# Layer norms of a decoder layer: four last slabs by token tile, scaled rows on ScalarE alone, an early split moved

## The reference

```python
h = layer_norm(ALPHA * h + 0.5 * swiglu(h, ffn1...), ln1_g, ln1_b)      # first norm
mix = hybrid_mixer(h, ...)      # projections, Mamba-2 branch, windowed attention, gates, w_out
h = layer_norm(ALPHA * h + mix, ln2_g, ln2_b)                            # second norm
h = layer_norm(ALPHA * h + 0.5 * swiglu(h, ffn2...), ln3_g, ln3_b)      # last norm

def layer_norm(x, g, b):
    mu = mean(x); xc = x - mu; var = mean(xc * xc)
    return xc * rsqrt(var + 1e-5) * g + b
def swiglu(x, w_gate, w_up, w_down):
    return (silu(x @ w_gate) * (x @ w_up)) @ w_down
```

## Time and profile before

| | us |
|---|---|
| median of 3 runs | 2670.36 |
| time of the profiled execution | 2668.99 |
| its span (first to last instruction) | 2667.4 |
| PE busy | 2634.5 (99%) |
| PE weight loads busy | 2188.8 (82%) |
| DVE busy | 2002.6 (75%) |
| ACT busy | 1361.7 (51%) |
| POOL busy | 130.0 (5%) |
| granted PE clock, mean | 0.996 |

### The profile page before, as it was taken

One profiled execution on the slowest core, in us unless ns is written; L12 is line 12 of the kernel. 1 busy time (PEld: TensorE's weight loads), 2 busy tenths in 40 slices (PEclk: granted clock), 3 DMA queues, 4 the chain that ended last, 5 costly groups with the idle time before them and its releaser, 6 DMA issues.

```text
span 2667.4 us, 36687 instructions
## 1 busy us (share of the span) xinstructions
PE 2634.5 (99%) x12546; PEld 2188.8 (82%) x12546; DVE 2002.6 (75%) x2410; ACT 1361.7 (51%) x1678; POOL 130.0 (5%) x170
## 2 busy tenths in 40 slices
PE   8999999999999999999999999999999999999997
PEld 7888888888787788888888888888878888888886
DVE  6999997688666665677777765444689999977986
ACT  5555555455344454566555554444355555554553
POOL 1000000000000000211111100000000000000000
PEclk9999999999999999999999999999999999999999
DMA  6666566666655546665555565667666665666664
GB/s 224 204 191 209 185 205 204 214 200 204 189 171 147 156 150 197 206 181 179 177 177 177 179 183 165 190 190 247 200 190 204 190 211 186 205 202 229 210 208 171
DMA packets 286195, 513.96 MB, mean 193 GB/s; under 512 B 19648, under 2 KB 52592, under 8 KB 284048
## 3 DMA queue, kind: packets, MB, share of 16 engines
q1 hardware_dynamic: 279552, 485.03, 57.8%
q0 software_dynamic: 4880, 25.36, 2.6%
q10 hardware_dynamic: 1664, 2.26, 0.2%
HBM read 506.23 MB, written 6.36 MB: 192 GB/s over the span
## 4 chain that ended last, share of the span: by engine, by line
PE 95%; DVE 3%; ACT 1%; issue 0%; DMA 0%; POOL 0%; POOLq 0%; SPq 0%; ACTq 0%; DVEq 0%
PE acc L787 13%; PE acc L789 13%; PE acc L788 13%; PE acc L853 5%; PE acc L855 5%; PE acc L854 5%; PE acc L871 4%; PE acc L872 4%; PE acc L873 4%; PE spare L871 4%; PE spare L872 4%; PE spare L873 4%; PE spare L855 3%; PE spare L854 3%; PE spare L853 3%; PE spare L756 2%
## 5 line engine op out<-in xcount | busy, mean ns | idle before, releaser
L1728 DVE TENSOR_TENSOR w_lo<-land,w_hi 128x1024 fp32r<-128x1024 f32 (+1 forms) x956 | 1149.2, 1219 | 499.4 <-ACT w_hi L1309 490.6
L1309 ACT ACTIVATE w_hi<-land 128x1024 fp32r<-128x1024 f32 (+1 forms) x956 | 976.8, 1029 | 916.9 <-PE acc L789 328.0
L787 PE MATMUL acc<-w_hi,a_hi 128*128 128x512 f32 (+1 forms) x1184 | 451.2, 381 | 2.6 <-DVE a_lo L1775 1.8
L789 PE MATMUL acc<-w_hi,a_lo 128*128 128x512 f32 (+1 forms) x1184 | 435.8, 368 | 0.0
L788 PE MATMUL acc<-w_lo,a_hi 128*128 128x512 f32 (+1 forms) x1184 | 434.4, 367 | 0.0
L787 PEld LDWEIGHTS acc<-w_hi,a_hi 128*128 128x128 f32 x1184 | 223.9, 189 | 46.8 <-issue 9.2
L789 PEld LDWEIGHTS acc<-w_hi,a_lo 128*128 128x128 f32 x1184 | 223.6, 189 | 38.2
L788 PEld LDWEIGHTS acc<-w_lo,a_hi 128*128 128x128 f32 x1184 | 224.1, 189 | 37.4 <-issue 3.6
L853 PE MATMUL acc<-w_hi,a_hi 128*128 128x512 f32 x576 | 227.7, 395 | 2.0 <-DVE a_lo L1775 1.7
L855 PE MATMUL acc<-w_hi,a_lo 128*128 128x512 f32 x576 | 225.1, 391 | 0.0
L854 PE MATMUL acc<-w_lo,a_hi 128*128 128x512 f32 x576 | 225.0, 391 | 0.0
(11 more groups left out here) (388 smaller groups left out, 4233.1 us busy)
## 6 DMA issues: line engine op xcount, KB each, us to landing
land<-w_in SPq DMA_DIRECT2D x232, 512.0 KB, 3.9
land<-ffn_w_gate SPq DMA_DIRECT2D x176, 512.0 KB, 3.9
land<-ffn_w_up SPq DMA_DIRECT2D x176, 512.0 KB, 4.3
land<-ffn_w_down SPq DMA_DIRECT2D x176, 512.0 KB, 4.7
land<-w_ssd_o SPq DMA_DIRECT2D x64, 512.0 KB, 4.3
land<-w_in SPq DMA_DIRECT2D x132, 128.0 KB, 2.3
land<-w_attn_o SPq DMA_DIRECT2D x32, 512.0 KB, 4.1
land<-w_out SPq DMA_DIRECT2D x32, 512.0 KB, 4.4
```

The costliest lines, as they stand in the source:

```text
L787: pe.matmul(to, rows_hi, hi, start=first, stop=False)
L789: mm = pe.matmul(to, rows_lo, hi, start=False, stop=last)
L1309: act.activation(w_hi[:, l % SPLIT, 0:deep, 0:width], land[:, l % LAND, 0:deep, 0:width], ACT.Copy).then_inc(high, 1)
L1728: dve.tensor_tensor(w_lo[:, l % SPLIT, 0:deep, 0:width], land[:, l % LAND, 0:deep, 0:width], w_hi[:, l % SPLIT, 0:deep, 0:width].bitcast(F ...
```

## The change

There are four edits.

1. `HALVED` goes from 3 to 4: the last four slabs of the last chunk of down1, out and down2 are gone through by token tile. In down1 and down2 the chunk's last four slabs are the last four of the stage (the four before them belong to the chunk beside it).
2. ACT's `ln_tile` with gain and bias writes the scaled rows into `sz` in float32 (two instructions), and then `a_hi` as a rounding copy of `sz` (one instruction of 128x512), with a wait of ACT for its own writes between them. From tile 2 on it first waits until DVE is done with tile u - 2, whose place in `sz` it takes.
3. DVE's `ln_tile` loses its two scaling instructions and the wait behind them, and takes `sz` as ACT wrote it. Before DVE uses `sz` for other things (`mixed_rows`) it waits for the end of its own tiles 6 and 7.
4. In `ln_first` the split of the next stage's first slab moves behind the normalising of tile 0.

```diff
-HALVED = 3
+HALVED = 4
...
@@ ln_tile of ACT
+                if u >= 2:
+                    read_bank(phase, 0, f"t{u - 2}")
+                h = sz[:, u % 2, :].rearrange("p (k n) -> p k n", k=2)
                 for k in range(2):
-                    last = act.activation(a_hi[:, 2 * u + k, :], two_tiles(bank)[:, k, :], ACT.Identity,
+                    last = act.activation(h[:, k, :], two_tiles(bank)[:, k, :], ACT.Identity,
                                           scale=ln_col[:, cols, 2 * u + k:2 * u + k + 1],
                                           bias=ln_col[:, cols + 1, 2 * u + k:2 * u + k + 1])
-                last.then_inc(tile_hi, 1)
+                ch.link(last)
+                act.activation(a_hi[:, 2 * u:2 * u + 2, :], h, ACT.Copy).then_inc(tile_hi, 1)
...
@@ ln_tile of DVE
                 h = sz[:, u % 2, :].rearrange("p (k n) -> p k n", k=2)
-                for k in range(2):
-                    last = dve.tensor_scalar(h[:, k, :], two_tiles(bank)[:, k, :],
-                                             ln_col[:, cols, 2 * u + k:2 * u + k + 1],
-                                             ln_col[:, cols + 1, 2 * u + k:2 * u + k + 1], ALU.mult, ALU.add)
-                ch.link(last)
                 dve.tensor_tensor(a_lo[:, at, :], h, a_hi[:, at, :].bitcast(F32), ALU.subtract
                                   ).then_inc(bank_out[bank], 1)
...
@@ ln_first of DVE
                     evacuate_half(phase, i, cc, scale, t, no)
+                    dve.wait_ge(ln_p, (no - 1) * TOK + t + 1)
+                    ln_part(t, 0)
+                    ln_part(t, 1)
                     if t == 0:
                         for l in range(EARLY_V):
                             split(after, 0, l)
-                    dve.wait_ge(ln_p, (no - 1) * TOK + t + 1)
-                    ln_part(t, 0)
-                    ln_part(t, 1)
...
@@ mixed_rows of DVE
                 read_done(ln, 0, f"t{u}")
+                if s == 0:
+                    read_done(ln, 0, "t6")
+                    read_done(ln, 0, "t7")
```

## The result

The changed kernel took 2678.87 us (median of 8 runs, 2677.12 to 2684.21); the kernel before took 2670.51 (8 runs). The ratio is 1.0034, with a 95% interval of 1.0025 to 1.0042: slower by 9 us. The forecast was 2669.3, and the time lies outside its range. The profiled execution took 2678.22 us, 9.2 more than that of before.

A forecast was written before the change was run, and what follows sets the result against it. PE was taken as the bound, busy 99% of the span, with only two norm gaps of about 4.4 us to win. Gains of 0.72 and 0.66, cut to 1.1 for the clock, took 2670.36 to 2669.3 us (range 2666.3 to 2671.8).

The forecast's parts named there:

- Parts 2 and 3: Both norms: with the scaling on ACT alone, `a_lo` comes 1.80 us behind ACT's start, not 2.16; gain 0.36 us each.
- the sum: Both norms together: 0.72 us at the first and 0.66 at the second, 1.38 us, taken as 1.1 after the clock.
- The rival on the slower side: ACT at both norms: a tile with its split takes over 3.2 us and PE follows ACT; up to 2679 us; chance 3%.
- ACT's wait for its own writes: ACT, between the scaling and the copy to `a_hi`: taken as 0.04 us, with 0.2 as the upper bound.
- the lag of 0.36: First norm: DVE started tile 1's evacuation 0.36 us later than PE's end allowed; removing this was the gain.
- At the second norm the same stretch: Second norm, to PE's first product: gain 0.3 us from DVE starting tile 1 sooner and 0.36 from the scaling, 0.66.
- PE's wait for `a_lo`: Sign at the first norm: this wait would be near 1.4 us instead of 1.80.
- out's last slabs: End of out: slab 31's `w_lo` ready 0.56 us ahead; rival that PE waits, at most some 0.7 us, 2669.9; chance 5%.
- The clock: Both norms: if its rise ignores PE's work, half the gain is lost; rival that it stays up, 2665.0 or 2667; chance 5%.
- my 0.7 to 1.4: Whole kernel: bounds of the gain in us, by whether the clock's rise stays put or moves with the work.
- one of my signs of being wrong: At the norms: the forecast is wrong if the clock's low stretch changes by more than 1 us.
- Parts 1 and 4: First norm: four slabs by token tile and the moved split let tile 1's evacuation start sooner; gain 0.36 us (0.3 to 0.43).

The follow-up runs named there:

- e1_fill16: The changed kernel with 16 one-column copies more on DVE, spread over the slabs of attn_o ahead of the ssd loop: 2667.74 us, ratio 0.9992.
- e3_parts23: The kernel before with the scaling on ACT alone, HALVED = 3 and the early split where it was: 2678.53 us, ratio 1.0034.
- e4_before_fill113: The kernel before with 113 one-column copies on DVE ahead of the slabs of attn_o, and none of the four edits: 2680.97 us, ratio 1.0043.
- e5_fill2: The changed kernel with 2 one-column copies on DVE ahead of the ssd loop: 2677.9 us, ratio 1.0031.
- e6_fill4: The changed kernel with 4 one-column copies on DVE ahead of the ssd loop: 2667.77 us, ratio 0.9992.
- e9_fill124: The changed kernel with 124 one-column copies on DVE ahead of the ssd loop: 2668.53 us, ratio 0.9996.
- e10_halved4: The kernel before with HALVED = 4 alone: 2668.86 us, ratio 0.9996.
- e13_in116: The kernel before with 116 one-column copies on DVE inside the body of the ssd loop: 2673.26 us, ratio 1.001.

## Why the prediction was wrong, point by point

**The step that failed.** Parts 2 and 3 took the 16 instructions that DVE loses at the first norm for time saved and nothing else ("now DVE saves 2 x 0.99 of scaling"), and the sum had no term for anything outside the norms and the ends of the stages. The missing term is the fetching of DVE's instructions: +11.2 us of PE's time in the profiled execution, shown by e1_fill16 (gone with 16 copies), e3_parts23 (there with that edit alone) and e4_before_fill113 (there without any edit). The Trainium skill has a rule for it ("Runtime: NRT & Kernel Launch", section "Instruction fetch mechanics"): a taken branch whose target isn't in the current window of two pages forces a fetch before execution can go on. The traces agree on the stall, 3.3 to 4.5 us here from the jump to the next instruction. It does not agree on the size of the pages for DVE: the section says 16 KB, 256 instructions, with room for two. The changed kernel and e4_before_fill113 begin their loop exactly 128 instructions apart against such pages, so in one of the two a body of 262 would reach only two of them and stay. Both stall. Here DVE's blocks are 8 KB (0.39 less 0.31 MB for ten), and it is the fourth that is too many.

Why the fourth is too many can be read from the packets, though they don't say which block they bring. In each of the five kernels with gaps there are five fetches from one jump to the next, for a body of four blocks, and the fifth comes 0.2 to 2.1 us before DVE starts the fourth block (in the changed kernel at 1445.52, where DVE starts it at 1446.80). So by the count a block behind the body was fetched before the jump. Where the body has three blocks, it and the one behind make four, and in the kernel before no fetch comes at all between the jumps. The reading that fits all runs is that four blocks stay and that the next is always fetched ahead.

**The rival on the slower side** was the wrong one: it had ACT as the bound. ACT has less room than before but enough. In the changed kernel, ahead of turned tiles 4 and 5:

```profile
729.60 1.02 ACT L1347 ACTIVATE sz<-spare,ln_col 128x256 f32<-128x256 f32 x2
730.66 0.63 ACT L1351 ACTIVATE a_hi<-sz 128x512 fp32r<-128x512 f32 x1
731.20 1.05 ACT L1309 ACTIVATE w_hi<-land 128x1024 fp32r<-128x1024 f32 x1
732.79 1.02 ACT L1347 ACTIVATE sz<-spare,ln_col 128x256 f32<-128x256 f32 x2 [0.55 <-PE spare L756]
```

The period of a tile is 3.19 us (732.79 less 729.60), PE's own, and 0.55 us of it is idle time. Ahead of tile 4 there is none now; before, there were 3.52 us. ACT's wait for its own writes costs what I took: the copy starts 0.04 us behind the end of the two instructions. No later tile makes PE wait.

**What held.** At the first norm the rows of the changed kernel are these, DVE first and then POOL:

```profile
713.11 0.69 DVE L1823 SCALAR_TENSOR_TENSOR resid<-acc,resid 128x512 f32<-128x512 f32 x1 [0.68 <-PE acc L873]
...
715.79 1.00 DVE L1839 TENSOR_SCALAR resid<-resid,mv,rstd 128x512 f32<-128x512 f32 x2 [0.96 <-POOL rstd L632]
716.71 1.22 DVE L1732 TENSOR_TENSOR w_lo<-land,w_hi 128x1024 fp32r<-128x1024 f32 x1
718.49 0.69 DVE L1823 SCALAR_TENSOR_TENSOR resid<-acc,resid 128x512 f32<-128x512 f32 x1 [0.56 <-PE acc L873]
...
721.14 1.00 DVE L1839 TENSOR_SCALAR resid<-resid,mv,rstd 128x512 f32<-128x512 f32 x2 [0.94 <-POOL rstd L632]
724.00 0.69 DVE L1774 TENSOR_TENSOR a_lo<-sz,a_hi 128x512 fp32r<-128x512 f32 x1 [1.86 <-ACT a_hi L1351]
```

```profile
714.92 0.18 POOL L631 TENSOR_TENSOR rstd<-mv,eps 128x1 f32<-128x1 f32 x1 [219.87 <-DVE mv L1835]
```

Tile 0's evacuation waits for PE for 0.68 us instead of 2.04, 1.36 sooner; POOL's first instruction takes 0.18 us and not 1.03; tile 1's evacuation starts 5.38 us behind tile 0's, where PE's pass is 5.44 us longer, so the lag of 0.36 is gone.

```profile
721.75 1.11 PE L756 MATMUL spare<-ident,resid 128*128 128x128 f32 x8 [2.42 <-DVE resid L1839]
724.75 0.79 PE L787 MATMUL acc<-w_hi,a_hi 128*128 128x512 f32 x1 [1.89 <-DVE a_lo L1774]
```

From PE's turns of tile 1 to its first product it is 3.00 us, where it was 3.37: the 0.36 us of the scaling. From PE's end to the first product it is 6.31 us where it was 7.09, and I had said about 6.4. At the second norm the same stretch is shorter by 0.95 us, where I had 0.66. One sign that I had named fails, though, PE's wait for `a_lo`: 1.89 us and not 1.4. In this execution the turns took 1.11 us at full clock instead of 1.57, so PE began to wait sooner. out's last slabs had their `w_lo` in time: there is no wait of PE there.

**The clock.** The sum went from 1.38 us down to 1.1, because the clock could take up to half. Five of the kernels have all four edits, so their profiled executions can be compared with that of before. Won in us, up to the first product of the next stage, and by the clock after it (first norm, second norm):

```
                 to first product     by the clock
changed            0.78, 0.95          0.48,  0.21
e5_fill2           0.78, 0.95          0.35,  0.19
e1_fill16          0.78, 0.95         -0.90, -0.84
e6_fill4           0.78, 0.95         -1.07, -1.02
e9_fill124         0.78, 0.95         -1.03, -0.86
```

Up to the first product all five win the same, 1.73 us where I had 1.38. What the clock adds or takes differs from one execution to the next, and my 0.7 to 1.4 do not bound it. By the windows, the low stretch at the first norm lasted 6.8 us before (721.86 to 728.68), 3.4 us in the changed kernel (724.28 to 727.68) and 6.8 us in e1_fill16 (723.24 to 730.06). A change of over 1 us was one of my signs of being wrong, and it came. The window from 728 to 729 on PE (us, busy (x), PEclk, DMA share, GB/s) shows the two cases, the changed kernel and then e1_fill16:

```profile
728.00:729.00 1.00, 1.00 (x6) 1.00 0.68 262
728.00:729.00 1.00, 1.00 (x3) 0.50 0.72 262
```

What decides between them these runs don't show.

**Parts 1 and 4 in the sum.** I priced them together at 0.36 us and named POOL's slow instruction as the reason for the move. e10_halved4 shows that the move has no part in the gain; I had not worked out either edit by itself.

**The kernel without the fault.** The changed kernel with 4 or with 16 copies took 2667.77 and 2667.74 us, both with a ratio of 0.9992 (0.9983 to 1.0001). This is 2.1 and 1.7 us under the kernel before, in an interval that still holds 1. The gain of 1.1 to 1.4 us that I forecast for the four edits is thus neither confirmed nor excluded by the times; the rows show the 1.73.

## What to carry to other kernels

Where DVE's program has a loop, an edit ahead of it moves the loop against the blocks in which the instructions are fetched, and the cost can show far from the edit, here 600 us. So count, for each loop, the instructions of a body and the place where it begins, before and after the change, and not only the edited ones. In this kernel the body in four blocks cost PE 4.8 to 6.3 us at each jump back, or 1.6 where it began far from a block's end. Two shorter loops of DVE, of 101 and 62 instructions, needed 0.2 to 0.3 us from each jump back in every kernel. Other engines were not tested. In a trace the sign is idle time whose releaser is "issue" right behind a jump, with more packets on the instruction queue; a few harmless instructions ahead of the loop tell in one run whether that is the cause (two were too few here, four enough).

## What the runs showed of the hardware that I had not expected

- DVE's instructions come in blocks of 8 KB, 128 instructions as far as e4_before_fill113 and the table of boundaries tell: bodies of 262 to 366 instructions within three blocks stayed (0.25 to 0.28 us from jump to next instruction, nine kernels), bodies of 262 to 378 that touched four did not (3.3 to 4.5 us, five kernels). The start of the body is not enough to tell, nor is its length alone.
- A further block that is wanted two or four instructions behind the jump costs another 1.4 to 2.7 us (four kernels); one wanted 117 instructions later costs nothing (e13_in116).
- Each such kernel fetched five blocks from one jump to the next, one more than its body has, and the fifth just before DVE got to the fourth. That four stay and the next is fetched ahead is inferred from the times of the packets.
- Two gaps of together 5 us on DVE, which is busy for 75% of the span, became 5.0 to 6.2 us on PE in the changed kernel, 3.1 of them as a wait and 1.7 to 3.0 at half clock.
